# The low halves of ten weight units move from VectorE to GpSimd in a hybrid decoder trunk on one Trainium2 core

## The chip, the cores and the metric

One core of a Trainium2 chip (trn2) runs the program. The metric is the device time of one execution in microseconds. All times below are microseconds unless marked ns. "Layer" is one of the two decoder layers, and a "unit" is one block of weights (see below).

## What is computed

A trunk of two layers over 512 tokens with 2048 features each. Every layer makes one wide projection of the normalised input, feeds three branches from it (latent attention with 6 heads, a convolution over 31 tokens, a state-space scan with 12 heads in chunks of 128), joins them, projects back and adds the input:

```python
def hybrid_layer(x, norm_g, w_in, ...):
    h = rms_norm(x, norm_g)
    u = h @ w_in
    c_q, c_kv, k_pe, g_mla, u_conv, g_conv, z, xbc, dt_raw = jnp.split(u, offs, axis=-1)
    o_mla = mla_mixer(c_q, c_kv, k_pe, ...) * jax.nn.silu(g_mla)
    o_conv = conformer_conv_mixer(u_conv, ...) * jax.nn.silu(g_conv)
    o_ssd = ssd_mixer(z, xbc, dt_raw, ...)
    y = jnp.concatenate([o_mla, o_conv, o_ssd], axis=-1) @ w_out
    return x + y

def ssd_chunked(x, dt, a_neg, bm, cm):
    a_cs = jnp.cumsum(dtc * a_neg.reshape(g, r), axis=2)
    seg = a_cs[:, :, :, None] - a_cs[:, :, None, :]
    decay = jnp.exp(jnp.where(causal[None, None, :, :, None, None], seg, -jnp.inf))
    cb = jnp.einsum('bclgn,bcsgn->bclsg', cc, bc)
    y_diag = jnp.einsum('bclsg,bclsgr,bcsgrp->bclgrp', cb, decay, xdt)
    ...
    return (y_diag + y_off).reshape(bsz, s, h, p)
```

All arrays are float32.

## The kernel before

**Weights.** All weights of a layer lie in memory as 126 units (`UNITS`, 0 to 125), in the order in which TensorE uses them. A full unit is 128x1024 float32, 512 KB. SyncE loads unit u into `stage[u % 2]` (L426). ScalarE copies it to `whi[u % 3]` in the format fp32r, its high half (`split` of ScalarE, L743). VectorE subtracts the two, `wlo = stage - whi`, the low half (`split` of VectorE, L1011). TensorE multiplies each block three times, high by high, high by low and low by high (`three`, L491 to L493), 24 matmuls to a unit.

**Semaphores of a unit.** `hi_done` counts ScalarE's copies, `lo_done` VectorE's subtractions, `unit_used` the units that TensorE has finished. SyncE loads unit u after the low half of unit u - 2, since they share a stage buffer. ScalarE copies unit u once unit u - 3 is used. TensorE begins unit u after its low half.

**Order of the work.** Each engine runs the same list `STEPS` in order, each with its own part of a step. The list is written out by `steps()`; a step has a name and the units that it owns. At a step that owns unit u, ScalarE and VectorE first split unit u + 3 (`split(u + RING)`), and then do what the name asks. Every engine is in order: an instruction that waits holds all that stands behind it on that engine.

**The scan steps.** After the attention, the two halves ("half 0", "half 1") of the projection tiles j = 27 to 35 take turns with the steps `ssd_a` and `ssd_b` of eight pieces s = 0 to 7 of the scan (two groups of heads, four chunks each):

```
in(27,0) unit 62 | ssd_a(0) | in(27,1) unit 63 | in(28,0) unit 64 | ssd_b(0) | ssd_a(1)
in(28,1) unit 65 | in(29,0) unit 66 | ssd_b(1) | ssd_a(2) | in(29,1) unit 67 | in(30,0) unit 68 | ssd_b(2) | ssd_a(3)
in(30,1) unit 69 | in(31,0) unit 70 | ssd_b(3) | ssd_a(4) | in(31,1) unit 71 | in(32,0) unit 72 | ssd_b(4) | ssd_a(5) ...
```

In `ssd_a(s)` each engine has a part:
- GpSimd waits for `ssd_in` of piece s - 1 (for s = 0: for `o_taken`, the last head of the attention), and issues a DMA that spreads six rows of running sums over 128 partitions into `acsb` (L463).
- ScalarE waits for that load (`acsb_loaded`), and makes `mt` from it with six Relu (L913), then small exponentials, `ecs`, a copy `btok`, and the exponential of `mt` (all L731).
- VectorE waits for the load too, makes `cols`, one step of the 31-tap convolution (`convolve`, L1066), `cbm`, `xdt`, `xw`, `ecs`, and last `mt` (L993), whose end is the signal `ssd_in` of piece s. That end is called E(s) below.
- TensorE turns blocks of `xb` (L657, L658, L496), which needs all five tiles of the group (`xb_ready`): `ssd_a(4)` needs the tile of in(30,1).

`ssd_b(s)` multiplies on TensorE (it waits for `ssd_in` of piece s) and adds up on VectorE. Tiles 26 to 30 are convolved over four tokens right after their second half: VectorE takes the tile out of PSUM into `raw`, ScalarE makes the first tap (L832), VectorE three more (L1002, `xb`), ScalarE a tanh into `temp` (L731), VectorE the product (L1002).

Of the kernel before, what the change touches and what calls it, by code (L numbers as in the profile page):

```python
# [19 lines left out]
F32 = mybir.dt.float32  # L20
F32R = mybir.dt.float32r
ALU = mybir.AluOpType
# [4 lines left out]
D_MODEL, SEQ, DEPTH = 2048, 512, 2  # L27
# [119 lines left out]
STEPS, UNITS = steps()  # L147
# [19 lines left out]
NU = len(UNITS)  # L167

TILE_UNIT = [UNITS.index(("in01", 3))] * 2 + [UNITS.index(("in", j, 1)) for j in range(2, len(TILES))] + [UNITS.index(("out2", 3))] * 2
TILE_UNIT += [UNITS.index(("out", f, 1)) for f in range(2, KX)]  # L170
STAGE, RING = 2, 3
assert NU % STAGE == 0 and NU % RING == 0


# [29 lines left out]
def hybrid_kernel(nc, x, weights, params, consts, out, acs_rows):  # L204
    ctx = ExitStack()
    with ctx:
# [25 lines left out]
        stage = [sb(f"stage{i}", [P, 1024]) for i in range(STAGE)]  # L232
        whi = [sb(f"whi{i}", [P, 1024], F32R) for i in range(RING)]
        wlo = [sb(f"wlo{i}", [P, 1024], F32R) for i in range(RING)]
# [82 lines left out]
        def sig(name, per_layer, credit=0):  # L317
            return Signal(nc, ctx, name, per_layer, credit)
# [13 lines left out]

        unit_used = sig("unit_used", NU, credit=RING)
        hi_done = sig("hi_done", NU)
        lo_done = sig("lo_done", NU, credit=STAGE)
        params_ready = sig("params_ready", 1)
        x_ready = sig("x_ready", KX, credit=KX)
        h_hi = sig("h_hi", 2 * KX)
# [72 lines left out]
        act_chain = sig("act_chain", 0)  # L411
        dve_chain = sig("dve_chain", 0)

        block = ctx.enter_context(nc.Block())


        @block.sync
        def _(sp):
            sp.dma_start(pvn[:, :], params[0:P, :]).then_inc(params_loaded.sem, 16)
            for layer in range(DEPTH):  # L420
                for name, args, own in STEPS:
                    for u in own:

                        sp.wait_ge(lo_done.sem, lo_done.at(layer, u - STAGE + 1))
                        src = weights[layer:layer + 1, STARTS[u]:STARTS[u + 1]].rearrange("o (p w) -> (o p) w", p=P)
                        sp.dma_start(stage[u % STAGE][:, 0:WIDTHS[u]], src).then_inc(stage_loaded[u % STAGE].sem, 16)  # L426
                        if layer == 0 and u == 3:
                            sp.dma_start(const[:, :], consts).then_inc(const_loaded.sem, 16)
                    if name == "out" and args == (2, 0) and layer < DEPTH - 1:

                        sp.wait_ge(ssd_taken.sem, ssd_taken.at(layer, 8))
                        sp.dma_start(pvn[:, :], params[layer * P + P:layer * P + 2 * P, :]).then_inc(params_loaded.sem, 16)
            sp.wait_ge(params_loaded.sem, params_loaded.at(DEPTH - 1, 0))


        @block.gpsimd
        def _(pool):
            pool.sem_inc(x_free.sem, 1)

            def go():  # L440

                pool.sem_inc(pool_go, 1)


            for layer in range(DEPTH):
                for name, args, own in STEPS:
                    if name == "acs_turn":
                        pool.wait_ge(acs48_ready.sem, acs48_ready.at(layer, 1))
                        go()
                        pool.dma_start(acs_rows, acs48).then_inc(acs_stored.sem, 16)  # L450
                        pool.wait_ge(acs_stored.sem, acs_stored.at(layer, 16))
                    if name == "ssd_a":
                        s = args[0]
                        g, c = s // NT, s % NT
                        if s == 0:

                            pool.wait_ge(o_taken.sem, o_taken.at(layer, HEADS))
                        else:

                            pool.wait_ge(ssd_in.sem, ssd_in.at(layer, s))  # L460
                        rows = acs_rows[12 * c + 6 * g:12 * c + 6 * g + 6, :].rearrange("(o h) l -> o (h l)", o=1)
                        go()
                        pool.dma_start(acsb[:, :, :].rearrange("p h l -> p (h l)"),  # L463
                                                      rows.to_broadcast([P, GH * P])).then_inc(acsb_loaded.sem, 16)
                    if name == "out2" and args[0] < 2 or name == "out" and args[1] == 0:
                        f = args[0]
                        if f == 0:

                            pool.wait_ge(ssd_taken.sem, ssd_taken.at(layer, 8))
                        if f >= 2:  # L470

                            pool.wait_ge(acc_taken.sem, acc_taken.at(layer, len(TILES) + f - 1))
                        go()
                        pool.dma_start(xr[f % 2][:, :], (out if layer else x)[:, f * SEQ:(f + 1) * SEQ]).then_inc(res_loaded[f % 2].sem, 16)
                        if f >= 2:
                            pool.wait_ge(x_ready.sem, x_ready.at(layer, f - 1))
                            go()
                            pool.dma_start(out[:, (f - 2) * SEQ:(f - 1) * SEQ], xg[:, f - 2, :]).then_inc(x_stored.sem, 16)
                for f in (KX - 2, KX - 1):
                    pool.wait_ge(x_ready.sem, x_ready.at(layer, f + 1))  # L480
                    go()
                    pool.dma_start(out[:, f * SEQ:(f + 1) * SEQ], xg[:, f, :]).then_inc(x_stored.sem, 16)

                pool.wait_ge(x_stored.sem, x_stored.at(layer, 16 * KX))
                pool.sem_inc(x_free.sem, 1)

        @block.tensor
        def _(pe):
# [13 lines left out]
            for layer in range(DEPTH):  # L502
# [6 lines left out]

                for name, args, own in STEPS:  # L510
                    for u in own:
                        pe.wait_ge(lo_done.sem, lo_done.at(layer, u + 1))
                    if name == "first":
                        quarter = args[0]
                        if layer and quarter == 0:
# [8 lines left out]
                    elif name == "in":  # L524
                        j, half = args
                        u, m = own[0], tile_columns(j)
# [38 lines left out]
                    elif name == "v":  # L565
                        hf, u = args[0], own[0]
# [43 lines left out]
                    elif name == "attend":  # L610
# [12 lines left out]
                        if 1 <= n <= 24:  # L623
# [4 lines left out]
                            for kb in range(m % 4 + 1):  # L628
                                b = slice(kb * P, kb * P + P)
# [16 lines left out]
                    elif name == "ssd_a":  # L646
# [8 lines left out]
                        b = slice(c * P, c * P + P)  # L655
# [28 lines left out]
                    elif name == "pw":  # L684
                        f, u = args[0], own[0]
# [10 lines left out]
                    elif name == "out2":  # L696
                        quarter, u = args[0], own[0]
# [12 lines left out]
                    elif name == "out":  # L710
                        f, half = args
                        u = own[0]
# [257 lines left out]
        def _(dve):  # L970
            nc.vector.memset(ones[:, :], 1.0).then_inc(first_set, 1)
            nc.vector.memset(eps_col[:, 0:1], NORM_EPS).then_inc(first_set, 1)
            nc.vector.memset(eps_col[:, 1:2], LN_EPS).then_inc(first_set, 1)
            dve.sem_inc(lo_done.sem, STAGE)
            dve.wait_ge(first_set, 3)
            dve.sem_inc(x_ready.sem, KX)

            for layer in range(DEPTH):
# [25 lines left out]
                def split(u, layer=layer):  # L1004
                    if u >= NU:
                        u, layer = u - NU, layer + 1
                    if layer == DEPTH:
                        return
                    dve.wait_ge(hi_done.sem, hi_done.at(layer, u + 1))
                    w = WIDTHS[u]  # L1010
                    nc.vector.tensor_tensor(wlo[u % RING][:, 0:w], stage[u % STAGE][:, 0:w],  # L1011
                                                       whi[u % RING][:, 0:w].bitcast(F32), ALU.subtract).then_inc(lo_done.sem, 1)
# [505 lines left out]
```

## Time and profile before

| | |
|---|---|
| median of 3 runs | 1608.91 (1607.62 to 1609.47) |
| span of the profiled execution, first to last instruction | 1604.2 |
| median of the runs less that span | 4.7 |
| mean granted TensorE clock, share of full speed | 0.990 |
| TensorE matmuls, busy | 1549.0 (97%) |
| VectorE, busy | 1009.8 (63%) |
| ScalarE, busy | 685.6 (43%) |
| GpSimd, busy | 44.6 (3%) |
| VectorE's subtractions of low halves (L1011), 252 | 300.6, mean 1197 ns |
| GpSimd's loads of `acsb` (L463), 16 | issue to landing 4.2 in the median |

The profiled execution has no time of its own beside its span; the runs above are other executions of the same program. Busy time is the sum of an engine's instructions; the pipelined matmuls overlap, and their ends are modelled. A row of the order of time gives start, length, engine, line, what is written and read, and in brackets the engine's idle time before it with what ended that. "POOL" is GpSimd, "PE" TensorE, "DVE" VectorE, "ACT" ScalarE, "SP" SyncE.

### The profile page before, as it was taken

How to read it: one execution, taken by the hardware profiler on the slowest of the kernel's cores; microseconds unless marked ns; L12 is line 12 of the kernel's file. 1: busy time of each engine (PE TensorE's matmuls, PEld its weight loads, DVE VectorE, ACT ScalarE, POOL GpSimd, SP SyncE). 2: the span in 40 equal slices, each digit the busy share in tenths (PEclk: the TensorE clock that was granted, in tenths of full speed). 3: DMA queues.
4: the chain of work that ended last, by engine and by line, in shares of the span. 5: the costliest groups of instructions: out<-in, count | busy, mean ns of one | idle time of the engine just before them, and what ended most of it. 6: DMA issues, size and time to landing. Idle time of an engine off the chain costs nothing.

```text
span 1604.2 us, 18430 instructions
## 1 busy us (share of the span) xinstructions
PE 1549.0 (97%) x7062; PEld 1233.2 (77%) x7062; DVE 1009.8 (63%) x1496; ACT 685.6 (43%) x1010; POOL 44.6 (3%) x86
## 2 busy tenths in 40 slices
PE   7999999999998999999999999999999899999997
PEld 5777777777776777888887877777777678778885
DVE  7545665889898666543464456668998985672231
ACT  7455443434445644212254455433444565351210
POOL 0000000000000000110000000000000000001100
PEclk9999999999999999999999999999999999999999
DMA  5332222222233313545432222222222332225442
GB/s 218 101 93 79 87 85 66 79 66 66 76 104 100 102 61 100 158 136 153 138 99 88 79 84 101 79 66 66 67 79 86 95 107 88 85 92 167 143 137 66
DMA packets 44423, 158.13 MB, mean 99 GB/s; under 512 B 5520, under 2 KB 5808, under 8 KB 44336
## 3 DMA queue, kind: packets, MB, share of 16 engines
q1 hardware_dynamic: 36720, 129.64, 24.9%
q0 software_dynamic: 6464, 23.12, 5.0%
q10 hardware_dynamic: 1152, 4.19, 0.7%
q8 instruction: 56, 0.92, 0.2%
q14 instruction: 31, 0.25, 0.1%
HBM read 148.50 MB, written 8.44 MB: 98 GB/s over the span
## 4 chain that ended last, share of the span: by engine, by line
PE 76%; DVE 14%; ACT 6%; issue 2%; DMA 1%; ACTq 0%; DVEq 0%; POOL 0%; POOLq 0%
PE acc L491 16%; PE acc L493 16%; PE acc L492 16%; PE S L496 5%; PE S L491 3%; PE S L493 3%; PE S L492 3%; PE T L493 2%; PE T L491 2%; PE T L492 2%; DVE wlo L1011 2%; ACT whi L743 2%; DVE xb L1002 2%; PE O L496 2%; PE T L630 1%
## 5 line engine op out<-in xcount | busy, mean ns | idle before, releaser
L491 PE MATMUL acc<-hhi,whi 128*128 128x512 f32 (+1 forms) x1504 | 603.7, 401 | 16.2 <-DVE wlo L1011 16.2
L1011 DVE TENSOR_TENSOR wlo<-stage,whi 128x1024 fp32r<-128x1024 f32 (+3 forms) x252 | 300.6, 1197 | 477.8 <-ACT whi L743 476.1
L493 PE MATMUL acc<-hhi,wlo 128*128 128x512 f32 (+1 forms) x1504 | 589.9, 392 | 0.0
L492 PE MATMUL acc<-hlo,whi 128*128 128x512 f32 (+1 forms) x1504 | 589.3, 392 | 0.0
L743 ACT ACTIVATE whi<-stage 128x1024 fp32r<-128x1024 f32 (+3 forms) x252 | 259.9, 1035 | 477.8 <-PE acc L493 261.0
L491 PEld LDWEIGHTS acc<-hhi,whi 128*128 128x128 f32 (+1 forms) x1504 | 283.8, 189 | 79.6 <-DVE wlo L1011 17.9
L492 PEld LDWEIGHTS acc<-hlo,whi 128*128 128x128 f32 (+1 forms) x1504 | 283.9, 189 | 61.6 <-issue 3.3
L493 PEld LDWEIGHTS acc<-hhi,wlo 128*128 128x128 f32 (+1 forms) x1504 | 283.1, 188 | 62.5
L1066 DVE SCALAR_TENSOR_TENSOR cacc<-glu,pv,cacc 128x512 f32<-128x512 f32 x240 | 171.5, 749 | 4.4
L731 ACT ACT_TABLE_LOAD x63 | 80.8, 1283 | 7.1 <-issue 4.9
L491 PE MATMUL S<-hhi,whi 128*128 128x512 f32 x192 | 75.2, 392 | 0.5 <-DVE wlo L1011 0.5
L731 ACT ACTIVATE prob<-S,cols 128x128 f32<-128x128 f32 (+3 forms) x48 | 25.4, 529 | 117.4 <-DVE cols L1270 117.4
L492 PE MATMUL S<-hlo,whi 128*128 128x512 f32 x192 | 74.7, 389 | 0.0
L493 PE MATMUL S<-hhi,wlo 128*128 128x512 f32 x192 | 74.7, 389 | 0.0
L491 PE MATMUL T<-hhi,whi 128*128 128x512 f32 x128 | 49.8, 389 | 0.0
L492 PE MATMUL T<-hlo,whi 128*128 128x512 f32 x128 | 49.8, 389 | 0.0
L493 PE MATMUL T<-hhi,wlo 128*128 128x512 f32 x128 | 49.8, 389 | 0.0
L1002 DVE SCALAR_TENSOR_TENSOR xb<-raw,pv,xb 128x512 f32<-128x512 f32 x60 | 45.1, 752 | 2.8
L496 PE MATMUL S<-qk 64*128 64x128 f32 (+7 forms) x128 | 45.9, 457 | 0.0
L491 PEld LDWEIGHTS S<-hhi,whi 128*128 128x128 f32 x192 | 36.0, 188 | 9.0 <-DVE wlo L1011 1.4
L492 PEld LDWEIGHTS S<-hlo,whi 128*128 128x128 f32 x192 | 36.0, 188 | 7.7 <-issue 0.2
L493 PEld LDWEIGHTS S<-hhi,wlo 128*128 128x128 f32 x192 | 36.0, 188 | 7.5
(229 smaller groups left out, 1560.0 us busy)
## 6 DMA issues: line engine op xcount, KB each, us to landing
stage<-weights SPq DMA_DIRECT2D x236, 512.0 KB, 3.4
y_features<-xg POOLq DMA_DIRECT2D x32, 256.0 KB, 4.2
acsb<-acs_rows POOLq DMA_DIRECT2D x16, 384.0 KB, 4.2
xg<-x_features ACTq DMA_DIRECT2D x8, 512.0 KB, 9.3
xr<-x_features POOLq DMA_DIRECT2D x16, 256.0 KB, 4.2
xr<-y_features POOLq DMA_DIRECT2D x16, 256.0 KB, 4.1
stage<-weights SPq DMA_DIRECT2D x8, 256.0 KB, 2.7
stage<-weights SPq DMA_DIRECT2D x4, 384.0 KB, 3.0
```

What stands on the lines that cost most here:

```text
L491: nc.tensor.matmul(out, a, c, start=start, stop=False)
L492: nc.tensor.matmul(out, a, d, start=False, stop=False)
L493: return nc.tensor.matmul(out, b, c, start=False, stop=stop)
L496: return nc.tensor.matmul(out, a, b, start=start, stop=stop)
L630: last = nc.tensor.transpose(T[m % 2][:, b], prob[m % 2][:, b], ident)
L731: nc.scalar.activation(out, in_, func, **more).then_inc(signal.sem, 1)
L743: nc.scalar.activation(whi[u % RING][:, 0:w], stage[u % STAGE][:, 0:w], ACT.Copy).then_inc(hi_done.sem, 1)
L1002: d(signal, nc.vector.scalar_tensor_tensor(out=out, in0=x, scalar=s, in1=y, op0=op0, op1=op1), go)
L1011: nc.vector.tensor_tensor(wlo[u % RING][:, 0:w], stage[u % STAGE][:, 0:w], whi[u % RING][:, 0:w].bitcast(F32), ALU.subtract).then_inc(lo_d ...
L1066: ins = nc.vector.scalar_tensor_tensor(out=cacc[:, j, :], in0=src, scalar=wt, in1=cacc[:, j, :], op0=ALU.mult, op1=ALU.add)
```

## The change

A table `POOL_LO` names units 65, 67, 69, 71 and 73, the second halves of tiles 28 to 32. Their subtraction leaves VectorE's `split` and is issued by GpSimd, in the same step in which VectorE did it (that of unit u - 3, so of units 62, 64, 66, 68 and 70), ahead of what GpSimd does for later steps. It waits for `hi_done` of its unit and counts up `pool_lo_done`. Who waited for `lo_done` (SyncE and TensorE) now asks `wait_lo`, which picks the semaphore by the unit. The credit of two on `lo_done` falls away, with the waits that used it up.

```diff
--- before.py
+++ after.py
@@ -169,6 +169,8 @@
 TILE_UNIT = [UNITS.index(("in01", 3))] * 2 + [UNITS.index(("in", j, 1)) for j in range(2, len(TILES))] + [UNITS.index(("out2", 3))] * 2
 TILE_UNIT += [UNITS.index(("out", f, 1)) for f in range(2, KX)]
 STAGE, RING = 2, 3
+
+POOL_LO = [UNITS.index(("in", j, 1)) for j in range(28, 33)]
 assert NU % STAGE == 0 and NU % RING == 0
 
 
@@ -332,7 +334,8 @@
 
         unit_used = sig("unit_used", NU, credit=RING)
         hi_done = sig("hi_done", NU)
-        lo_done = sig("lo_done", NU, credit=STAGE)
+        lo_done = sig("lo_done", NU - len(POOL_LO))
+        pool_lo_done = sig("pool_lo_done", len(POOL_LO))
         params_ready = sig("params_ready", 1)
         x_ready = sig("x_ready", KX, credit=KX)
         h_hi = sig("h_hi", 2 * KX)
@@ -411,6 +414,17 @@
         act_chain = sig("act_chain", 0)
         dve_chain = sig("dve_chain", 0)
 
+        def wait_lo(engine, layer, u):
+
+            if u < 0:
+                u, layer = u + NU, layer - 1
+            if layer < 0:
+                return
+            if u in POOL_LO:
+                engine.wait_ge(pool_lo_done.sem, pool_lo_done.at(layer, POOL_LO.index(u) + 1))
+            else:
+                engine.wait_ge(lo_done.sem, lo_done.at(layer, u + 1 - sum(v < u for v in POOL_LO)))
+
         block = ctx.enter_context(nc.Block())
 
 
@@ -421,7 +435,7 @@
                 for name, args, own in STEPS:
                     for u in own:
 
-                        sp.wait_ge(lo_done.sem, lo_done.at(layer, u - STAGE + 1))
+                        wait_lo(sp, layer, u - STAGE)
                         src = weights[layer:layer + 1, STARTS[u]:STARTS[u + 1]].rearrange("o (p w) -> (o p) w", p=P)
                         sp.dma_start(stage[u % STAGE][:, 0:WIDTHS[u]], src).then_inc(stage_loaded[u % STAGE].sem, 16)
                         if layer == 0 and u == 3:
@@ -444,6 +458,12 @@
 
             for layer in range(DEPTH):
                 for name, args, own in STEPS:
+                    for u in own:
+                        if u + RING in POOL_LO:
+                            b = (u + RING) % RING
+                            pool.wait_ge(hi_done.sem, hi_done.at(layer, u + RING + 1))
+                            nc.gpsimd.tensor_tensor(wlo[b][:, :], stage[(u + RING) % STAGE][:, :], whi[b][:, :].bitcast(F32),
+                                                    ALU.subtract).then_inc(pool_lo_done.sem, 1)
                     if name == "acs_turn":
                         pool.wait_ge(acs48_ready.sem, acs48_ready.at(layer, 1))
                         go()
@@ -509,7 +529,7 @@
 
                 for name, args, own in STEPS:
                     for u in own:
-                        pe.wait_ge(lo_done.sem, lo_done.at(layer, u + 1))
+                        wait_lo(pe, layer, u)
                     if name == "first":
                         quarter = args[0]
                         if layer and quarter == 0:
@@ -971,7 +991,6 @@
             nc.vector.memset(ones[:, :], 1.0).then_inc(first_set, 1)
             nc.vector.memset(eps_col[:, 0:1], NORM_EPS).then_inc(first_set, 1)
             nc.vector.memset(eps_col[:, 1:2], LN_EPS).then_inc(first_set, 1)
-            dve.sem_inc(lo_done.sem, STAGE)
             dve.wait_ge(first_set, 3)
             dve.sem_inc(x_ready.sem, KX)
 
@@ -1004,7 +1023,7 @@
                 def split(u, layer=layer):
                     if u >= NU:
                         u, layer = u - NU, layer + 1
-                    if layer == DEPTH:
+                    if layer == DEPTH or u in POOL_LO:
                         return
                     dve.wait_ge(hi_done.sem, hi_done.at(layer, u + 1))
                     w = WIDTHS[u]
```

GpSimd's instructions from the attention to the end of the scan in one layer, before (numbered buffers are told apart by their suffix; `acs_rows` is stored much earlier in the layer, by `acs_turn`):

```order
L436 UNCONDITIONAL_BRANCH [waits barrier_Pool_Activation_PE_DVE_SP_gather]
L450 DMA acs_rows<-acs_94 48x128 [waits acs48_ready]
L463 DMA acsb<-acs_rows 128x768 [waits acs_stored,o_taken]
L463 DMA acsb<-acs_rows 128x768 [waits ssd_in] x7
L474 DMA xr_103<-x_features 128x512 [waits ssd_taken]
```

The same stretch with the change (lines are those of the changed kernel, 19 to 20 more than before on these engines):

```order
L470 DMA acs_rows<-acs_94 48x128 [waits acs48_ready]
L465 ISA
L465 TENSOR_TENSOR wlo_60<-stage_54,whi_57 128x1024 [waits hi_done,acs_stored]
L483 DMA acsb<-acs_rows 128x768 [waits o_taken]
L465 TENSOR_TENSOR wlo_59<-stage_54,whi_56 128x1024 [waits hi_done]
L483 DMA acsb<-acs_rows 128x768 [waits ssd_in]
L465 TENSOR_TENSOR wlo_58<-stage_54,whi_55 128x1024 [waits hi_done]
L483 DMA acsb<-acs_rows 128x768 [waits ssd_in]
L465 TENSOR_TENSOR wlo_60<-stage_54,whi_57 128x1024 [waits hi_done]
L483 DMA acsb<-acs_rows 128x768 [waits ssd_in]
L465 TENSOR_TENSOR wlo_59<-stage_54,whi_56 128x1024 [waits hi_done]
L483 DMA acsb<-acs_rows 128x768 [waits ssd_in] x4
```

Each of the first five loads of `acsb` now stands behind a subtraction that waits for `hi_done`; the subtractions belong to units 65, 67, 69, 71 and 73 in this order. The last three loads follow one another as before. One ISA instruction is new ahead of the first subtraction, in the first layer alone.

VectorE at the step of unit 64, between the last instruction of tile 27 and the start of `ssd_a(1)`, before:

```order
L1002 SCALAR_TENSOR_TENSOR xb_87<-temp_69,xb_87 128x512 [waits tanh_done]
L1011 TENSOR_TENSOR wlo_59<-stage_54,whi_56 128x1024 [waits hi_done,xb_ready]
L1066 SCALAR_TENSOR_TENSOR cacc<-glu,pv,cacc 128x512 [waits tap_done] x2
L1320 COPY state<-S 128x384 [waits ssd_y]
L1002 SCALAR_TENSOR_TENSOR xg<-xb_86,pv,S 128x128 [waits dve_chain]
L1002 SCALAR_TENSOR_TENSOR xg<-xb_86,pv,S 128x128 x2
L993 TENSOR_TENSOR cols<-acsb,small 128x6 [waits acs_ready,ssd_y,acsb_loaded,ssd_taken]
```

and with the change:

```order
L1021 SCALAR_TENSOR_TENSOR xb_87<-temp_69,xb_87 128x512 [waits tanh_done]
L1085 SCALAR_TENSOR_TENSOR cacc<-glu,pv,cacc 128x512 [waits tap_done,xb_ready]
L1085 SCALAR_TENSOR_TENSOR cacc<-glu,pv,cacc 128x512 [waits tap_done]
L1339 COPY state<-S 128x384 [waits ssd_y]
L1021 SCALAR_TENSOR_TENSOR xg<-xb_86,pv,S 128x128 [waits dve_chain]
L1021 SCALAR_TENSOR_TENSOR xg<-xb_86,pv,S 128x128 x2
L1012 TENSOR_TENSOR cols<-acsb,small 128x6 [waits acs_ready,ssd_y,acsb_loaded,ssd_taken]
```

The subtraction for unit 67 (`wlo_59`) is gone with its wait for `hi_done`, and the two convolution steps follow the product at once. The same row falls away at the steps of units 62, 66, 68 and 70.

## Rows read from the trace of the kernel before

**Rows 1.** The page: span, and busy time of each engine.
```profile
span 1604.2 us, 18430 instructions
...
PE 1549.0 (97%) x7062; PEld 1233.2 (77%) x7062; DVE 1009.8 (63%) x1496; ACT 685.6 (43%) x1010; POOL 44.6 (3%) x86
```

**Rows 2.** Busy time in stretches; columns: stretch, its length, each engine, granted clock, DMA.
```profile
core 0: us, PE busy (x) PEld busy (x) DVE busy (x) ACT busy (x) POOL busy (x), PEclk, DMA share, GB/s
...
465.00:480.00 15.00, 13.97 (x81) 11.26 (x80) 14.09 (x25) 7.71 (x15) 0.54 (x1) 1.00 0.29 97
...
490.00:492.00 2.00, 0.00 (x0) 0.00 (x0) 1.93 (x4) 0.84 (x2) 0.00 (x0) 0.85 0.48 197
...
494.00:496.00 2.00, 2.00 (x6) 1.53 (x5) 2.00 (x6) 0.60 (x3) 0.00 (x0) 0.50 0.39 59
...
498.00:500.00 2.00, 2.00 (x9) 1.59 (x9) 2.00 (x3) 0.99 (x2) 0.00 (x0) 0.95 0.00 0
```

**Rows 3.** What TensorE waited for, 425 to 600 us: total, times, longest.
```profile
PE T L657 <- DVE xb L1002: 5.0, 1, 5.0
```

**Rows 4.** VectorE in order of time: start, length, line, out<-in, idle before.
```profile
439.10 0.96 DVE L993 TENSOR_TENSOR mt<-mt,cbm 128x768 f32<-128x768 f32 x1 [0.23 <-ACT mt L731]
...
447.24 1.23 DVE L1011 TENSOR_TENSOR wlo<-stage,whi 128x1024 fp32r<-128x1024 f32 x1 [0.47 <-ACT whi L743]
448.38 1.41 DVE L1066 SCALAR_TENSOR_TENSOR cacc<-glu,pv,cacc 128x512 f32<-128x512 f32 x2
...
451.19 0.17 DVE L993 TENSOR_TENSOR cols<-acsb,small 128x6 f32<-128x6 f32 x1
...
484.94 0.95 DVE L993 TENSOR_TENSOR mt<-mt,cbm 128x768 f32<-128x768 f32 x1
```

**Rows 5.** ScalarE in order of time.
```profile
428.96 1.06 ACT L743 ACTIVATE whi<-stage 128x1024 fp32r<-128x1024 f32 x1
434.79 1.87 ACT L913 ACTIVATE mt<-acsb,small 128x128 f32<-128x128 f32 x6 [4.77 <-DMA acsb<-acs_rows]
...
446.08 1.06 ACT L743 ACTIVATE whi<-stage 128x1024 fp32r<-128x1024 f32 x1
447.04 1.85 ACT L913 ACTIVATE mt<-acsb,small 128x128 f32<-128x128 f32 x6
...
491.79 1.06 ACT L743 ACTIVATE whi<-stage 128x1024 fp32r<-128x1024 f32 x1
```

**Rows 6.** GpSimd in order of time.
```profile
430.99 0.56 POOL L463 DMA_DIRECT2D acsb<-acs_rows  x1 [271.44 <-DVE xg L993]
440.63 0.54 POOL L463 DMA_DIRECT2D acsb<-acs_rows  x1 [9.08 <-DVE mt L993]
```

**Rows 7.** The chain of waits in order of time: start, length, what.
```profile
430.39 0.03 POOLq L442
...
430.99 3.77 DMA acsb<-acs_rows
```

**Rows 8.** The loads of acsb in both layers, from issue to landing.
```profile
DMA to landing us min/median/max: 3.4/4.2/5.0
```

**Rows 9.** TensorE in order of time, one scan step.
```profile
470.52 0.45 PE L496 MATMUL S<-mt,xdt 128*64 128x128 f32 x4 [1.03 <-DVE mt L993]
...
484.13 0.39 PE L493 MATMUL acc<-hhi,wlo 128*128 128x512 f32 x1
```

**Rows 10.** The chain of waits around the end of the fourth step.
```profile
492.54 0.90 PE T L657 x3
...
506.98 1.65 PE S L496 x14
```

**Rows 11.** VectorE in the second layer, in order of time.
```profile
1228.90 0.96 DVE L993 TENSOR_TENSOR mt<-mt,cbm 128x768 f32<-128x768 f32 x1 [0.23 <-ACT mt L731]
...
1274.75 0.95 DVE L993 TENSOR_TENSOR mt<-mt,cbm 128x768 f32<-128x768 f32 x1
```

**Rows 12.** The page: all table loads of ScalarE.
```profile
L731 ACT ACT_TABLE_LOAD x63 | 80.8, 1283 | 7.1 <-issue 4.9
```

## The prediction

> **What bounds the kernel now.** I read the page first: TensorE's matmuls fill 97% of a span of 1604.2, VectorE is at 63%, GpSimd at 3% [rows 1]. That average says little about the change, which sits in the scan steps, so I read those 60 us next. The busy times by stretch show VectorE at 14.09 of 15 us there [rows 2], and the list of TensorE's waits has one of 5.0 for VectorE's `xb` [rows 3]. Between 430 and 492 the scan steps therefore go at VectorE's pace, and TensorE falls in with it. Then I laid the three orders of time beside each other.
>
> Measure the pace by E(s), the end of VectorE's `mt` of piece s. E(0) is 439.10 + 0.96 = 440.06, E(3) is 484.94 + 0.95 = 485.89 [rows 4]. Three periods take 45.83, or 15.28 each. One period's work on TensorE starts at 470.52 and ends at 484.13 + 0.39 [rows 9], 14.0, so TensorE has 1.3 to spare. The stretch ends when TensorE gets its last tile of `xb` at 492.54; from there it works without a gap to `ssd_b(4)` at 506.98 [rows 10], and everything later hangs on that. A shift of E(3) is therefore a shift of the end, one for one. The second layer is the same: 1228.90 + 0.96 to 1274.75 + 0.95, 45.84 [rows 11].
>
> GpSimd's part is small but not beside the point. For piece 0 it was released at 430.39, issued the load of `acsb` at 430.99, and the load landed 3.77 later, at 434.76 [rows 7]. ScalarE had waited 4.77 for it [rows 5]. For piece 1 the load was issued at 440.63, right behind E(0) [rows 6], so by 447.04 ScalarE found it there and began its Relu with no wait [rows 5]. That early issue is what keeps the load off the path in the periods after piece 0.
>
> **What is removed.** VectorE loses five subtractions a layer. The one for unit 67 began at 447.24 after an idle 0.47 for ScalarE's copy, and the next instruction began at 448.38 [rows 4]. Its removal frees 0.47 + 1.14 = 1.61. If nothing else changed, three such steps (units 67, 69 and 71) would bring E(3) forward by 4.8. The subtraction for unit 65 stood before the landing of a load that VectorE waited for anyway, and that for unit 73 lies behind the last `xb`; both give nothing.
>
> **What is added, and what stands behind it.** GpSimd is in order. Its load for piece s now stands behind the subtraction of a unit whose high half ScalarE makes in the same step, just ahead of its own Relu for that piece. The load that was issued 7 us before its use is now asked for when its use is due. Step by step, for a period from E(s) to E(s+1):
>
> 1. E(0) to the end of ScalarE's copy of unit 67, 446.08 + 1.06 = 447.14 [rows 5]: 7.08. All of it hangs on VectorE's `mt`, through the other subtraction, the tile and its taps.
> 2. GpSimd's subtraction of 128x1024. No row shows GpSimd at such work. The nearest row is VectorE's own, 1.23 [rows 4]; that is the lower end. I take twice that, 2.46, since an engine that must fetch two operands through one door makes two passes; the upper end is twice again, 4.92.
> 3. From GpSimd free to the load landed: 0.60 to the issue [rows 7], and the median 4.2 to the landing [rows 8], 4.80. The ends are 4.37, as for piece 0 [rows 7], and 5.6 with the longest landing of 5.0 [rows 8].
> 4. From the landing at 434.76 to E(0) at 440.06, with ScalarE's six Relu, exponentials and copy, and VectorE's `mt` in one row: 5.30. Piece 0 is the one piece where the load came last, so this is the right row for all.
>
> The period becomes 7.08 + 2.46 + 4.80 + 5.30 = 19.64. VectorE would be at `cols` 1.61 before its old 451.19 [rows 4], at 449.6, and finds the load missing until 447.14 + 2.46 + 4.80 = 454.4, so the freed time falls into a new wait. Three periods take 58.92 in place of 45.83: 13.09 more.
>
> Piece 0: the copy of unit 65 ends at 428.96 + 1.06 = 430.02 [rows 5], the subtraction at 432.48. GpSimd was ready to issue at 430.39, so the load comes 2.09 later.
>
> Piece 4: the copy of unit 73 ends at 491.79 + 1.06 = 492.85 [rows 5]; add 2.46, 4.80 and 5.30 and E(4) is at 505.41 on the old scale. TensorE asks for it at 506.98. This one is hidden with 1.6 to spare; without that cover its price is what lies over the margin. Loads 5 to 7 have no subtraction ahead of them.
>
> The rest costs nothing. SyncE's load of unit 69 waits for the low half of 67, which comes some 2.5 after its high half, and its own use lies a period away. TensorE needs unit 67 after E(1), by when it is long there. The two credits fall away before the first unit. TensorE idles 19.64 - 14.0 = 5.6 a period. In the trace it stood idle for the 5.0 before 492.54 [rows 3, 10]. Its granted clock was down to 0.85 in the mean of 490 to 492, at 0.50 from 494, and at 0.95 again from 498 [rows 2], that is 1.2 GHz instead of 2.4 for about 6 us, a loss of 3. Then a period's work is 17.0, still under 19.64.
>
> **Sum.** 13.09 + 2.09 = 15.18 a layer, 30.4 for both. The span of 1604.2 becomes 1634.6. The median of the runs stands 4.7 over the span, so the median becomes 1608.9 + 30.4 = **1639.3**.
>
> One page speaks of item 2. The Trainium skill, GPSIMD Engine Reference, Performance versus the Vector engine, gives 4497 ns for a float32 `tensor_tensor` add of 128x2048 on GpSimd; half of it, 2.25, is an estimate for this size, and by it the sum would be 28.7 and the median 1637.6. No row here shows it.
>
> **The rivals.**
>
> *A. VectorE's relief wins (faster).* VectorE is 94% busy in these steps [rows 2], and each period has 1.61 to give. If the load of `acsb` landed before VectorE's new arrival at `cols`, the gain is 4.8 a layer, 9.7 in all: 1599.2. The point that decides is the sum of items 2 and 3. With the old pace it must stay under 15.28 - 7.08 - 5.30 = 2.90. Item 3 alone took 4.37, and with the shortest landing of 3.4 [rows 8] it is 4.0. Even a subtraction that takes no time leaves the steps slower than before. Only a load that goes out ahead of its place in GpSimd's order could save it. 0.04.
>
> *B. GpSimd and VectorE stand in each other's way (slower still).* When ScalarE's copy ends, VectorE is in its two convolution steps, which took 1.41 [rows 4], and it has three or four short instructions behind them. With the subtraction gone it runs through all of them and stands still where `cols` was at 451.19 [rows 4], less 1.61, so at 449.6. If the subtraction has to wait until then, item 2 grows by 2.4, a layer by 7.3 and piece 4 by 0.9 over its margin: 16.4 in all, 1655.7. The other direction costs nothing, for VectorE has 5 us to lose. The Trainium skill, SBUF — State Buffer, Who interferes with whom, says that a VectorE instruction with two SBUF inputs and a GpSimd instruction that reads SBUF exclude each other, and that the one issued later waits. By that rule GpSimd waits at least for the convolution step in progress, a few tenths. No row of the trace before can show it. 0.20.
>
> *C. TensorE's clock becomes the bound.* If it stayed at 1.2 GHz through the whole period, 14.0 would become 28.0, 8.4 over the new period, 25 a layer, 50 in all: some 1690. Against it stands the return to 0.95 at 498, about 6 us after work resumed [rows 2]. 0.05.
>
> *D. No change that can be told.* Slower by less than 0.2% would need a period cheaper than its cheapest bound. 0.04 for a mistake of mine in what is queued behind what.
>
> The ISA instruction ahead of the first subtraction may be a load of code. If it is done when GpSimd reaches it, 270 us before its use, it is free; if it is done at the first subtraction, the nearest row is ScalarE's table load of 1283 ns [rows 12], once. I leave it out of the sum.
>
> **How the numbers follow.** My forecast has 0.67, B 0.20, C 0.05, A 0.04, D 0.04. Slower: 0.67 + 0.20 + 0.05 = 0.92; faster 0.04; within 0.2%, about what a measurement of this kernel can tell from no change, 0.04. Low end of the range: items 2 and 3 at 1.23 and 4.37, a period of 17.98, a layer of 3 x 17.98 - 45.83 + 0.86 = 9.0, 18 in all: 1627. At the high end a subtraction of 4.92 gives a layer of 4.55 + 20.5 + 0.9 over the margin, 25.9, or 1660.7; I stop at 1658, which holds B.
>
> **What would show it.** In the changed kernel's profile: E(0) to E(3) near 59, not 46 (items 1 to 4 can be read off one by one); GpSimd's idle time before its loads gone, and a subtraction of about 2.5 in front of each of five; ScalarE's Relu and VectorE's `cols` each waiting for the DMA of `acsb` some 5 to 7 us in pieces 1 to 4, where only piece 0 had such a wait; TensorE idle about 5 us a period for `mt`, with the granted clock down; nothing changed outside 430 to 507 and its twin in the second layer. The prediction is wrong if the loads are issued before the subtractions end, or if the Relu of piece 1 starts without a wait.

## The result and the profile after

The changed kernel takes 1633.88 (median of 4 runs, 1632.47 to 1634.59) against 1608.86 before (also 4 runs, one more than in the table above): a ratio of 1.0155, interval 1.014 to 1.017. It is slower by 25.0; the forecast was 30.4, and its range of 1627 to 1658 holds the time. The page of the changed kernel, answering to [rows 1]:

```profile
span 1631.1 us, 18433 instructions
...
PE 1557.7 (96%) x7062; PEld 1241.0 (76%) x7062; DVE 1020.8 (63%) x1486; ACT 685.4 (42%) x1010; POOL 69.6 (4%) x96
```

The span grew by 26.9. VectorE's share is where it was, GpSimd's went from 3% to 4%. The list of TensorE's waits from 425 to 600 (columns as in [rows 3]) has a new first line; the wait for `xb` that led it is shorter than its old 5.0:

```profile
PE S L516 <- DVE mt L1012: 12.2, 3, 6.1
PE T L677 <- DVE xb L1021: 3.8, 1, 3.8
```

Now the four steps of a period. GpSimd in order of time, beside [rows 6]: the two pieces 0 and 1, each a subtraction (L465) and behind it the load of `acsb` (L483).

```profile
431.89 2.37 POOL L465 TENSOR_TENSOR wlo<-stage,whi 128x1024 fp32r<-128x1024 f32 x1 [272.24 <-ACT whi L763]
434.22 0.59 POOL L483 DMA_DIRECT2D acsb<-acs_rows  x1
451.25 2.58 POOL L465 TENSOR_TENSOR wlo<-stage,whi 128x1024 fp32r<-128x1024 f32 x1 [16.44 <-ACT whi L763]
453.77 0.55 POOL L483 DMA_DIRECT2D acsb<-acs_rows  x1
```

ScalarE, beside [rows 5]: the copies of units 65 and 67, and the Relu of pieces 0 and 1. Before, only the first Relu waited for its load.

```profile
430.68 1.06 ACT L763 ACTIVATE whi<-stage 128x1024 fp32r<-128x1024 f32 x1
438.81 1.87 ACT L933 ACTIVATE mt<-acsb,small 128x128 f32<-128x128 f32 x6 [7.07 <-DMA acsb<-acs_rows]
...
450.10 1.06 ACT L763 ACTIVATE whi<-stage 128x1024 fp32r<-128x1024 f32 x1
458.21 1.86 ACT L933 ACTIVATE mt<-acsb,small 128x128 f32<-128x128 f32 x6 [7.06 <-DMA acsb<-acs_rows]
```

VectorE, beside [rows 4]: `mt` of piece 0, two convolution steps, `cols` and `mt` of piece 1, and `mt` of piece 3.

```profile
443.12 0.96 DVE L1012 TENSOR_TENSOR mt<-mt,cbm 128x768 f32<-128x768 f32 x1 [0.23 <-ACT mt L751]
...
450.82 3.55 DVE L1085 SCALAR_TENSOR_TENSOR cacc<-glu,pv,cacc 128x512 f32<-128x512 f32 x2
...
458.27 0.17 DVE L1012 TENSOR_TENSOR cols<-acsb,small 128x6 f32<-128x6 f32 x1 [2.53 <-issue]
...
462.51 0.96 DVE L1012 TENSOR_TENSOR mt<-mt,cbm 128x768 f32<-128x768 f32 x1 [0.23 <-ACT mt L751]
...
501.46 0.96 DVE L1012 TENSOR_TENSOR mt<-mt,cbm 128x768 f32<-128x768 f32 x1 [0.22 <-ACT mt L751]
```

E(0) is 443.12 + 0.96 = 444.08, E(1) 463.47, E(3) 502.42. Item by item, for the period from E(0) to E(1), with the items as the prediction numbers them:

| item | forecast | measured |
|---|---|---|
| 1. E(0) to the end of the copy of unit 67 (450.10 + 1.06) | 7.08 | 7.08 |
| 2. from there to the start of the load's instruction (453.77) | 2.46 | 2.61 |
| 3. from there to ScalarE's Relu (458.21) | 4.80 | 4.44 |
| 4. Relu to E(1) | 5.30 | 5.26 |
| period | 19.64 | 19.39 |
| E(0) to E(3) | 58.9 | 58.34 (before 45.83) |

The load went out 453.77 - 444.08 = 9.69 behind E(0), where it had been 440.63 - 440.06 = 0.57 [rows 4, 6]. ScalarE stood still for it 7.06 to 7.18 in pieces 1 to 4 of the first layer, VectorE at `cols` 2.0 to 3.3. The landing itself was like before, in the line of all 16 loads, beside [rows 8]:

```profile
DMA to landing us min/median/max: 4.1/4.4/4.6
```

### The profile page after: what moved, and what is told of

Read it like the earlier page. It is cut to its first block, busy times and chain, and to the rows that moved or that the text cites. A ratio compares the mean times of both kernels' runs of the same rounds, so it can differ in the third digit from the quotient of the medians.

```text
span 1631.1 us, 18433 instructions
## 1 busy us (share of the span) xinstructions
PE 1557.7 (96%) x7062; PEld 1241.0 (76%) x7062; DVE 1020.8 (63%) x1486; ACT 685.4 (42%) x1010; POOL 69.6 (4%) x96
## 4 chain that ended last, share of the span: by engine, by line
PE 74%; DVE 9%; issue 8%; ACT 5%; DMA 1%; POOL 1%; ACTq 0%; DVEq 0%; POOLq 0%
PE acc L511 16%; PE acc L513 16%; PE acc L512 16%; PE S L516 5%; PE S L511 3%; PE S L513 3%; PE S L512 3%; PE T L513 2%; PE T L512 2%; PE T L511 2%; DVE wlo L1030 2%; PE O L516 2%; ACT whi L763 1%; PE T L650 1%; ACT L751 1%
## 5 line engine op out<-in xcount | busy, mean ns | idle before, releaser
L1030 DVE TENSOR_TENSOR wlo<-stage,whi 128x1024 fp32r<-128x1024 f32 (+3 forms) x242 | 288.4, 1196 | 464.2 <-ACT whi L763 461.1
L1085 DVE SCALAR_TENSOR_TENSOR cacc<-glu,pv,cacc 128x512 f32<-128x512 f32 x240 | 192.3, 836 | 4.7
L933 ACT ACTIVATE mt<-acsb,small 128x128 f32<-128x128 f32 x96 | 29.9, 390 | 75.4 <-DMA acsb<-acs_rows 73.5
L465 POOL TENSOR_TENSOR wlo<-stage,whi 128x1024 fp32r<-128x1024 f32 x10 | 25.4, 2538 | 673.2 <-ACT whi L763 673.2
L516 PE MATMUL S<-mt,xdt 128*64 128x128 f32 x192 | 23.7, 337 | 23.5 <-DVE mt L1012 23.4
```

The lines of the kernel that those rows point to most:

```text
L465: nc.gpsimd.tensor_tensor(wlo[b][:, :], stage[(u + RING) % STAGE][:, :], whi[b][:, :].bitcast(F32), ALU.subtract).then_inc(pool_lo_done.se ...
L516: return nc.tensor.matmul(out, a, b, start=start, stop=stop)
L933: nc.scalar.activation(mt[:, h, :], acsb[:, h, :], ACT.Relu, scale=-1.0, bias=one).then_inc(seg_pos.sem, 1)
L1085: ins = nc.vector.scalar_tensor_tensor(out=cacc[:, j, :], in0=src, scalar=wt, in1=cacc[:, j, :], op0=ALU.mult, op1=ALU.add)
```

## The experiments

Two theories stood against each other. **Q**: the loss is one of order; GpSimd's loads of `acsb` stand behind a wait that ends late. **S**: GpSimd's subtraction is slow in itself, wherever it stands. Besides, the runs were to tell how much relief VectorE's work could give, and whether GpSimd and VectorE hold each other up.

| run | E(0) to E(3) | median | ratio to before |
|---|---|---|---|
| before | 45.83 | 1608.9 | |
| the change | 58.34 | 1633.9 | 1.0155 (1.014 to 1.017) |
| 1 load first | 47.55 | 1608.7 | 1.0001 (0.9989 to 1.0013) |
| 2 wait only | 51.41 | 1616.0 | 1.0056 (1.0038 to 1.0074) |
| 3 left out | 41.10 | 1599.4 | 0.9946 (0.9927 to 0.9965) |
| 4 memset | 41.12 | 1591.7 | 0.9903 (0.9885 to 0.9921) |
| 5 two halves, fitted | 42.68 | 1601.5 | 0.9959 (0.9947 to 0.9972) |
| 6 three parts, fitted | 41.16 | 1591.5 | 0.9901 (0.9886 to 0.9916) |

Each ratio is against runs of the kernel before that were made along with it; their median is 1609.3 for runs 1 to 4 and 1608.6 for runs 5 and 6. E(0) to E(3) is read in each profile from the two `mt` rows of the first layer; in the second layer it is within 0.1 of that (57.92 for the change, 0.4 less). It is the steadier measure: the clock of TensorE, which comes and goes at a few other places, does not enter it.

### 1. The load first, the subtraction behind it

```diff
                     for u in own:
-                        if u + RING in POOL_LO:
-                            b = (u + RING) % RING
-                            pool.wait_ge(hi_done.sem, hi_done.at(layer, u + RING + 1))
+                        if u + 2 in POOL_LO:
+                            b = (u + 2) % RING
+                            pool.wait_ge(hi_done.sem, hi_done.at(layer, u + 2 + 1))
...
```

The subtraction that follows takes its buffers by u + 2 as well.

> The changed kernel with one thing moved: GpSimd does each of the five subtractions one step later in its own order, so that the load of acsb of the piece is issued right behind E(s), as before the change, and the subtraction comes after it. Same work on every engine. Theory Q (the queue order is the cause of the loss): E(0) to E(3) falls from 58.3 to near the old 45.8 and the Relu of pieces 1 to 4 waits for no load. Inside it two sub-theories. Q with exclusion (two-input work of VectorE and GpSimd keep each other out; in the changed kernel's trace the two convolution steps took 3.55 in place of 1.41): a period is 15.4 - 1.6 + 2.1 = 15.9, E(0) to E(3) 47.4, the whole 1612, slightly slower than before. Q without exclusion: 13.8 a period, 41.0, the whole 1599. Theory S (GpSimd's slow subtraction itself is the cause, whatever its place): 1630 or more.

Measured: 1608.72, no different from the kernel before. GpSimd and VectorE in order of time:

```profile
441.56 0.58 POOL L483 DMA_DIRECT2D acsb<-acs_rows  x1 [6.29 <-DVE mt L1012]
448.14 2.60 POOL L465 TENSOR_TENSOR wlo<-stage,whi 128x1024 fp32r<-128x1024 f32 x1 [6.00 <-ACT whi L763]
```

```profile
440.01 0.96 DVE L1012 TENSOR_TENSOR mt<-mt,cbm 128x768 f32<-128x768 f32 x1 [0.23 <-ACT mt L751]
...
447.73 3.56 DVE L1085 SCALAR_TENSOR_TENSOR cacc<-glu,pv,cacc 128x512 f32<-128x512 f32 x2
...
487.57 0.95 DVE L1012 TENSOR_TENSOR mt<-mt,cbm 128x768 f32<-128x768 f32 x1
```

The load goes out at 441.56, 0.6 behind E(0), and E(0) to E(3) is 487.57 + 0.95 - 440.97 = 47.55, against a forecast of 47.4 with exclusion and 41.0 without. The whole loss of 25 is gone with the same five subtractions on GpSimd. Theory S has fallen. But the relief did not come either: two convolution steps took 3.56 in place of 1.41 [rows 4], just when GpSimd subtracted (448.14 to 450.74). 2.15 more and 1.61 less leave 0.54 a period, and three of them 1.6; measured 1.7.

### 2. The wait alone

```diff
                 for name, args, own in STEPS:
+                    for u in own:
+                        if u + RING in POOL_LO:
+                            pool.wait_ge(hi_done.sem, hi_done.at(layer, u + RING + 1))
                     if name == "acs_turn":
```

This is the kernel before with one wait more, five times a layer; the table `POOL_LO` is the one of the change.

> The kernel before, with nothing moved to GpSimd; only GpSimd waits for the high half of units 65, 67, 69, 71 and 73 at the places where the change puts the subtractions, ahead of the loads of acsb. Theory Q: the wait alone takes most of the loss. Period 7.1 to the high half, 0.6 + 4.3 for issue and load, 5.3 to E: 17.3, so E(0) to E(3) 51.9 instead of 45.8, nothing for piece 0, 6.1 a layer, 12 in all: 1621. Theory S: no subtraction, no loss: 1609.

Measured: 1616.04, slower with no work moved. VectorE's `mt` of pieces 0 and 3, and ScalarE's Relu of piece 1:

```profile
439.50 0.96 DVE L997 TENSOR_TENSOR mt<-mt,cbm 128x768 f32<-128x768 f32 x1 [0.23 <-ACT mt L735]
...
490.91 0.96 DVE L997 TENSOR_TENSOR mt<-mt,cbm 128x768 f32<-128x768 f32 x1 [0.23 <-ACT mt L735]
```

```profile
452.32 1.87 ACT L917 ACTIVATE mt<-acsb,small 128x128 f32<-128x128 f32 x6 [4.77 <-DMA acsb<-acs_rows]
```

E(0) to E(3) is 491.87 - 440.46 = 51.41, forecast 51.9. The Relu waits 4.77 for a load that before had landed in time. So of the 12.5 that the change adds from E(0) to E(3), the wait for the high half makes 5.6; the remaining 6.9, 2.3 in each of three periods, is the length of a subtraction in front of the load; behind the load, in experiment 1, it delays no load. By ScalarE's copies the scan steps cost 11.5 in the two layers (5.7 and 5.8), as forecast, and the stretches behind them in the first layer gave some 3 of it back: the copies stand 6.1 later at unit 72 and 3.2 at the layer's end. The profiled span is 9.8 longer than before; the ratio of the runs says 6 to 12.

### 3. The subtractions left out

```diff
-                engine.wait_ge(pool_lo_done.sem, pool_lo_done.at(layer, POOL_LO.index(u) + 1))
+                engine.wait_ge(hi_done.sem, hi_done.at(layer, u + 1))
```

and GpSimd's five subtractions a layer are deleted; the low half of these units is whatever lies in the buffer.

> The changed kernel with the five subtractions a layer left out altogether (units 65, 67, 69, 71, 73 are multiplied with whatever low half lies in the buffer); TensorE and SyncE wait for the high half of these units instead. This is the most that relieving VectorE can bring. Theory that VectorE sets the pace of the scan steps: 1.6 in each of three periods, E(0) to E(3) 41.0, 4.8 a layer, 9.7 in all: 1599, give or take 3 for TensorE's clock. Rival, that something else comes last at once (TensorE's own 14.0 a period): E(0) to E(3) 42 to 44 and 1603 to 1607.

Measured: 1599.36. VectorE: `mt` of piece 0, the two convolution steps, `mt` of piece 3.

```profile
441.01 0.96 DVE L1006 TENSOR_TENSOR mt<-mt,cbm 128x768 f32<-128x768 f32 x1 [0.23 <-ACT mt L745]
...
448.71 1.41 DVE L1079 SCALAR_TENSOR_TENSOR cacc<-glu,pv,cacc 128x512 f32<-128x512 f32 x2
...
482.12 0.95 DVE L1006 TENSOR_TENSOR mt<-mt,cbm 128x768 f32<-128x768 f32 x1
```

483.07 - 441.97 = 41.10: three times 1.58, as forecast (41.0). VectorE does set the pace of these steps, and 1.6 a period is there to be had; the rival of 42 to 44 has fallen.

### 4. GpSimd writes, but reads nothing

```diff
-                            nc.gpsimd.tensor_tensor(wlo[b][:, :], stage[(u + 2) % STAGE][:, :], whi[b][:, :].bitcast(F32),
-                                                    ALU.subtract).then_inc(pool_lo_done.sem, 1)
+                            nc.gpsimd.memset(wlo[b][:, :].bitcast(F32), 0.0).then_inc(pool_lo_done.sem, 1)
```

This is experiment 1, against which the cut stands, with the low half of the five units set to zero.

> As the first run of this group, but GpSimd only writes zeros into the low half of the five units (memset of 128x1024) in place of the subtraction, so it reads nothing from SBUF. If GpSimd's reads are what keeps VectorE's two-input work out: the convolution pair keeps its 1.41 and the time comes to that of the run that leaves the subtractions out, near 1599. If any GpSimd work on SBUF does it: the pair is longer by about the memset's length, and the time lies between 1599 and 1612.

GpSimd's memset, and VectorE's two convolution steps beside it with `mt` of pieces 0 and 3:

```profile
449.44 0.95 POOL L465 MEMSET wlo<- 128x1024 f32 x1 [6.01 <-ACT whi L762]
```

```profile
441.35 0.96 DVE L1011 TENSOR_TENSOR mt<-mt,cbm 128x768 f32<-128x768 f32 x1 [0.23 <-ACT mt L750]
...
449.05 1.42 DVE L1084 SCALAR_TENSOR_TENSOR cacc<-glu,pv,cacc 128x512 f32<-128x512 f32 x2
...
482.48 0.95 DVE L1011 TENSOR_TENSOR mt<-mt,cbm 128x768 f32<-128x768 f32 x1
```

The pair takes 1.42 while GpSimd writes 128x1024 values for 0.95. E(0) to E(3) is 483.43 - 442.31 = 41.12, that of the run with nothing in its place. So GpSimd's being at work does not hold VectorE up, nor does its writing; what is left is its reading. A GpSimd instruction that reads one tensor instead of two was not run. The Trainium skill, SBUF — State Buffer, Who interferes with whom, says just this: two SBUF inputs on VectorE collide with a GpSimd instruction that reads SBUF, not with one that only writes. By these two traces it holds.

The median of 1591.7 is 7.7 under that of experiment 3, although the scan steps are as long in both layers. The profiled spans are 2.9 apart (1593.9 and 1596.8). ScalarE's copies of the same unit, laid side by side, show where: 1.0 comes before unit 3 of the first layer, and 2.1 in the second layer, 0.8 of it in piece 0 and 1.4 behind unit 73. At that last place TensorE waited 3.4 for its `xb` in experiment 3 and the clock fell to half; in experiment 4 it waited 1.1 and the clock stayed up. Near the start of attention each of the two lost 1.6 at half clock, in one layer. The profiled execution of experiment 4, 1595.99, is also the slowest of its four, so the rest of the 7.7 is in executions without a profile read here, and stays open.

### 5. Two halves, started where VectorE reads PSUM

GpSimd keeps units 67, 69 and 71 only, always behind the load. Each part waits for a count of VectorE's convolution steps (`tap_done`). The cut is against the change; `PARTS` gives for each part how many steps late it comes, its first and last column, and which convolution step it waits for.

```diff
-POOL_LO = [UNITS.index(("in", j, 1)) for j in range(28, 33)]
+POOL_LO = [UNITS.index(("in", j, 1)) for j in range(29, 32)]
+PARTS = ((0, 0, 512, 0), (0, 512, 1024, 1))
...
+                        for late, first, end, taps in PARTS:
+                            v = u + 2 - late
+                            if v in POOL_LO:
+                                b, s = v % RING, (v - 65) // 2
+                                if taps is None:
+                                    pool.wait_ge(lo_done.sem, lo_done.at(layer, v + 2 - sum(x < v + 1 for x in POOL_LO)))
+                                else:
+                                    pool.wait_ge(hi_done.sem, hi_done.at(layer, v + 1))
+                                    pool.wait_ge(tap_done.sem, tap_done.at(layer, 97 + 5 * s + taps))
+                                nc.gpsimd.tensor_tensor(wlo[b][:, first:end], stage[v % STAGE][:, first:end],
+                                                        whi[b][:, first:end].bitcast(F32),
+                                                        ALU.subtract).then_inc(pool_lo_done.sem, 1)
```

> A version that is to beat both. GpSimd takes only units 67, 69 and 71 (the three whose removal shortens a period; 65 and 73 go back to VectorE), always behind the load of the piece, in two halves of 128x512. Each half waits for a count of VectorE's convolution steps so that it begins when VectorE turns to instructions with one SBUF input (the other is PSUM): the first half beside the product of the state, S and xg (about 1.4 without a second SBUF input), the second beside cbm and xdt (0.8). Theory X (only VectorE work with two SBUF inputs is kept out by a GpSimd read): the pair of convolution steps stays at 1.41, a half takes 1.2, the second half holds xw up by about 0.5, so a period is 15.4 - 1.6 + 0.5 = 14.4, 3 a layer, 6 in all: 1603. Theory Y (GpSimd at work slows VectorE whatever it reads): a gain of 1.6 is paid back with 2.4, a period of 16.2 and 1613.

Measured: 1601.52. GpSimd's two halves for unit 69, and VectorE's convolution pair and `xw` in the same period, between `mt` of piece 0 and of piece 3:

```profile
463.31 1.48 POOL L472 TENSOR_TENSOR wlo<-stage,whi 128x512 fp32r<-128x512 f32 x1 [6.92 <-DVE cacc L1093]
466.12 1.29 POOL L472 TENSOR_TENSOR wlo<-stage,whi 128x512 fp32r<-128x512 f32 x1 [1.34 <-DVE cacc L1093]
```

```profile
440.28 0.96 DVE L1020 TENSOR_TENSOR mt<-mt,cbm 128x768 f32<-128x768 f32 x1 [0.23 <-ACT mt L759]
...
461.74 1.41 DVE L1093 SCALAR_TENSOR_TENSOR cacc<-glu,pv,cacc 128x512 f32<-128x512 f32 x2
...
466.67 1.16 DVE L1020 TENSOR_TENSOR xw<-xdt,cols 128x384 f32<-128x384 f32 x1
...
482.98 0.94 DVE L1020 TENSOR_TENSOR mt<-mt,cbm 128x768 f32<-128x768 f32 x1
```

The pair is back at 1.41. The first half starts beside VectorE's `state<-state,cols` (463.07 to 463.62), which reads SBUF alone, and takes 1.48 where one beside a copy out of PSUM took 1.29; the rest of it lies beside PSUM work, and VectorE is not delayed. The second runs from 466.12 to 467.41, past the end of `cbm` and `xdt`, and `xw` takes 1.16 instead of 0.56. E(0) to E(3) is 483.92 - 441.24 = 42.68 (forecast 43.2).

### 6. Three parts

The cut is against experiment 5.

```diff
-PARTS = ((0, 0, 512, 0), (0, 512, 1024, 1))
+PARTS = ((2, 768, 1024, None), (0, 0, 512, 0), (0, 512, 768, 1))
```

The last quarter waits for VectorE's own subtraction of the next unit, behind which VectorE takes `raw` out of PSUM.

> As the run with two halves, but the second half is cut again: columns 512 to 768 beside cbm and xdt (0.8), columns 768 to 1024 one period later beside raw, which VectorE reads from PSUM, behind its own subtraction of the next unit. Theory X: hardly any of VectorE's two-input work is met, a period comes to 13.9 as in the run that left the subtractions out, 4.8 a layer: 1599 to 1601. What may spoil it: the last quarter is ready only 2 us after E, TensorE needs unit 67 some 3 us after E, and with a period of 13.9 TensorE's own 14.0 is the bound. Theory Y: 1613 or more, worse than two halves.

Measured: **1591.45, 17 faster than before and 42 faster than the change**. GpSimd: two parts of unit 69, the load of the next piece, the last part of unit 69.

```profile
462.04 1.47 POOL L472 TENSOR_TENSOR wlo<-stage,whi 128x512 fp32r<-128x512 f32 x1 [6.13 <-DVE cacc L1093]
464.85 0.74 POOL L472 TENSOR_TENSOR wlo<-stage,whi 128x256 fp32r<-128x256 f32 x1 [1.34 <-DVE cacc L1093]
468.32 0.56 POOL L491 DMA_DIRECT2D acsb<-acs_rows  x1 [2.73 <-DVE mt L1020]
469.03 0.73 POOL L472 TENSOR_TENSOR wlo<-stage,whi 128x256 fp32r<-128x256 f32 x1 [0.15 <-DVE wlo L1038]
```

VectorE: `mt` of piece 0, `xw`, `mt` of piece 3.

```profile
439.49 0.96 DVE L1020 TENSOR_TENSOR mt<-mt,cbm 128x768 f32<-128x768 f32 x1 [0.23 <-ACT mt L759]
...
465.40 0.60 DVE L1020 TENSOR_TENSOR xw<-xdt,cols 128x384 f32<-128x384 f32 x1
...
480.66 0.95 DVE L1020 TENSOR_TENSOR mt<-mt,cbm 128x768 f32<-128x768 f32 x1
```

`xw` is down to 0.60, and 481.61 - 440.45 = 41.16 is the 41.1 of leaving the work out. The subtractions now cost nothing.

That explains 4.7 a layer, some 9 in all; the run gained 17. Most of the rest is TensorE's clock. Its wait for the last tile of `xb`, the chain from there to `ssd_b(4)`, and a stretch of that time (columns as in [rows 2]):

```profile
PE T L685 <- DVE xb L1029: 3.0, 1, 3.0
```

```profile
488.22 0.55 PE T L685 x3
...
499.99 1.65 PE S L524 x14
```

```profile
488.00:492.00 4.00, 3.78 (x20) 3.27 (x21) 3.15 (x7) 2.66 (x7) 0.00 (x0) 1.00 0.22 47
```

Before, TensorE waited 5.0 at this place, came back at half clock for some 6 us, and needed 14.44 to `ssd_b(4)` [rows 2, 10]. Here it waited 3.0, the granted clock stayed at 2.4 GHz, and it needed 11.77: 2.7 saved. Against the trace of before, the high half of each unit is made 4.3 earlier at unit 72 (counted from 0), 7.0 at unit 75 and 8.6 at unit 88 of the first layer. The last 1.6 is the place described below. In the second layer the gain is 6.6, to 15.2 in all. There the clock did fall behind a shorter wait for the same `xb`:

```profile
1269.16 0.90 PE L685 MATMUL T<-const,xb 128*128 128x128 f32 x3 [2.71 <-DVE xb L1029]
```

```profile
1269.16:1272.00 2.84, 2.84 (x10) 2.55 (x11) 2.14 (x3) 2.35 (x7) 0.00 (x0) 0.50 0.01 3
```

The 15.2 is what the two spans are apart; the profiled execution of before lies some 2.7 below its median (see below), which makes most of the difference to 17.

## Why the prediction was right, and where it was off

**Right, by its own steps.** The mechanism is the one named: the load of `acsb` behind a subtraction that waits for a copy made just ahead of its use. Experiment 2 shows the wait's part without any moved work, experiment 1 takes the loss away with all work moved. The freed 1.61 of VectorE was real (experiment 3) and fell into a new wait. All four items held within 0.4, E(0) to E(3) within 0.6.

**Sizes that came near for another reason.** Item 2 doubled VectorE's 1.23 because of "two passes" through one door. No run tests that reason, so the size is in part luck: undisturbed the subtraction took 2.37, and 2.58 with 0.2 of waiting for VectorE. Item 3 counted 0.60 from GpSimd free to the issue. It did not come: the load's instruction begins at 453.77, just before the subtraction ends at 451.25 + 2.58 = 453.83, and 4.44 is left of the 4.80. Two signs were too large. VectorE was to wait some 5 to 7 at `cols` and waited 2.0 to 3.3, because it had lost 2.1 before, in its convolution pair. TensorE was to idle about 5 a period and idled 6.1, 3.3 and 2.8, because behind the first of these waits it worked at half clock for part of each period.

**Piece 0.** The copy of unit 65 began at 430.68, 1.72 later than before [rows 5]; TensorE had lost that at half clock between 240 and 243, a place the change does not touch, where other runs show it or not. Counted from there, E(0) moved by 444.08 - 440.06 - 1.72 = 2.30; the sum had 2.09.

**Piece 4** was hidden, as forecast. TensorE went from its last `xb` to `ssd_b(4)` without a wait (the chain, beside [rows 10]), in 13.4 where it had needed 14.4. E(4) was at 521.93, 0.6 ahead of that use, where the forecast left 1.6:

```profile
509.18 0.90 PE T L677 x3
...
522.60 1.65 PE S L516 x14
```

**Rival B had the interplay the wrong way round.** GpSimd waited hardly at all: 2.56 to 2.59 with VectorE in a convolution step at its start, 2.37 for the one subtraction of that layer that began beside a PSUM instruction, so about 0.2. It was VectorE that stood still, 3.55 for a pair of 1.41. In the change that cost nothing, since VectorE was ahead of the load. In experiment 1, where the load is in time, it is all that is left, and it eats the gain. The prediction priced this direction at nothing, which was right for the change alone.

**Rival C** did not come. The granted clock fell to half in each of the new waits, but TensorE had its work done before the next E.

**Two terms were off.** The scan steps cost 14.9 and 14.4 in the two layers by the times of ScalarE's copies, 29.3; the sum had 30.4. One step of the prediction failed, "nothing changed outside 430 to 507": the clock changed there. TensorE waits 2.4 for the low half of the first `pw` unit in both kernels; behind that gap the clock fell before, and did not fall after. Before, then after:

```profile
585.00:590.00 5.00, 3.31 (x8) 2.61 (x9) 3.96 (x6) 1.46 (x3) 0.00 (x0) 0.70 0.43 150
```

```profile
600.00:605.00 5.00, 2.71 (x12) 2.26 (x13) 3.91 (x7) 2.06 (x3) 0.00 (x0) 1.00 0.31 101
```

By ScalarE's copies that gave back 1.6 in the first layer and 1.4 in the second, and the shorter `xb` wait another 1.0 in the first and 0.1 in the second; against it stand the 1.7 lost near 240. This makes the 26.9 of the spans. The forecast had none of these terms; together they take off 2.4.

The other was "the median of the runs stands 4.7 over the span". In the runs of the changed kernel time and span of one execution lie 1.8 to 2.1 apart. The profiled execution of before was thus not a median one but some 2.7 below it, that of the change 0.7. That is 2.0, and with it 26.9 becomes 25.0.

No cost of loading code showed: GpSimd's first subtraction began 0.15 after ScalarE's copy had ended.

**Open.** Why the clock falls behind a gap of 2.4 in one trace and not in another was not settled, nor what part of the 7.7 between experiments 3 and 4 it makes. Whether units 65 and 73 could be moved without cost in the form of experiment 6 was not tried.

## What to carry to other kernels

Work given to an idle engine takes with it the engine's order. Ask what already stands in that queue, when it went out, and whether the new work's wait ends after that: a wait in front of an early request costs even with no work behind it. Put the request first. Then ask what the receiving engine shares with the one relieved: here a subtraction on GpSimd held up VectorE's two-input instructions for almost its whole length, and paid only when it was cut to fit beside instructions that read PSUM.

## What was not expected of the hardware

- GpSimd's subtraction of 128x1024 float32 took 2.37 to 2.60, of 128x512 1.29 undisturbed, of 128x256 0.73. Cutting it in three costs some 0.4 of GpSimd's time, which is free here.
- When both want to read, the lengths fit with GpSimd coming in at the end of VectorE's running instruction (2.58 against 2.37) and VectorE's next two-input one waiting for GpSimd to finish: pairs of 3.52 to 3.56 instead of 1.41 in eight of eight such meetings read in the first layers of the change and of experiment 1.
- A small gain at the right wait was nearly doubled by the clock. TensorE's gap of 5.0 before the last `xb` cost 2.7 more at 1.2 GHz; gaps of 3.7 to 4.4 in the first layers of experiments 1, 3, 4 and 5 also had the clock down behind them; the gap of 3.0 in experiment 6 did not. The length of the gap alone does not tell: the gap of 2.7 in that run's second layer had the clock at 0.50 behind it, and gaps of 2.4 went both ways.
